# Two-block model on one core: the first panel of each feed-forward as an ordinary product

## The reference

```
x = x + nsa_pool_mixer(rmsnorm(x))        # attention in three branches, multiscale pooling, w_out
x = x + swiglu(rmsnorm(x), w_gate, w_up, w_down)                  # feed-forward 1
x = x + conformer_conv(rmsnorm(x))        # 31-tap depthwise convolution, layernorm, silu
x = x + swiglu(rmsnorm(x), ...)                                   # feed-forward 2
x = rmsnorm(x)
x = x + gla_and_short_conv(rmsnorm(x))    # gated linear attention in chunks, 3-tap convolution
x = x + swiglu(rmsnorm(x), ...)                                   # feed-forward 3
x = x + sigmoid(rmsnorm(x) @ w_ple_gate) * (p @ w_ple_proj);  out = rmsnorm(x)
swiglu(h) = (silu(h @ w_gate) * (h @ w_up)) @ w_down              # 1024 -> 2816 -> 1024
```

## Time and profile before

| | us |
|---|---|
| time before, median of 3 runs | 1819.22 (1817.42 to 1821.11) |
| the profiled execution's own time | 1818.26 |
| its span, first to last instruction | 1816.5 |
| TensorE busy | 1727.3 (95%) |
| VectorE busy | 1284.4 (71%) |
| ScalarE busy | 882.8 (49%) |
| GpSimd busy | 557.9 (31%) |
| mean granted TensorE clock, share of full | 0.973 |

### The profile page before, as it was taken

One profiled execution on the slowest core, in us unless ns is written; L12 is line 12 of the kernel. 1 busy time (PEld: TensorE's weight loads), 2 busy tenths in 40 slices (PEclk: granted clock), 3 DMA queues, 4 the chain that ended last, 5 costly groups with the idle time before them and its releaser, 6 DMA issues.

```text
span 1816.5 us, 28182 instructions
## 1 busy us (share of the span) xinstructions
PE 1727.3 (95%) x10884; PEld 1503.3 (83%) x10884; DVE 1284.4 (71%) x1818; ACT 882.8 (49%) x1368; POOL 557.9 (31%) x392
## 2 busy tenths in 40 slices
PE   7989988999999999988999999999998899999997
PEld 6767778988998865778988998788777898899876
DVE  8667687754775798787754876678868775477575
ACT  5328566732673312556732673432246674277342
POOL 1332124512540246234502540024502451255000
PEclk9899999999999999989999999999998999999998
DMA  6210223433333465222433332322211343333322
GB/s 213 79 47 2 70 59 81 117 103 93 107 87 100 120 156 146 70 70 73 114 105 104 94 102 85 122 70 70 90 50 49 92 115 96 93 111 90 113 88 75
DMA packets 284702, 169.04 MB, mean 93 GB/s; under 512 B 8288, under 2 KB 278528, under 8 KB 284576
## 3 DMA queue, kind: packets, MB, share of 16 engines
q1 hardware_dynamic: 283664, 165.10, 32.4%
q0 software_dynamic: 624, 1.67, 0.3%
q10 hardware_dynamic: 288, 0.54, 0.1%
HBM read 156.59 MB, written 2.10 MB: 87 GB/s over the span
## 4 chain that ended last, share of the span: by engine, by line
PE 84%; DVE 10%; ACT 3%; issue 3%; DMA 1%; POOL 0%; SPq 0%; DVEq 0%; ACTq 0%; POOLq 0%
PE ps L1324 36%; PE ps L1012 13%; PE ps L1013 13%; PE ps L1014 13%; PE ps L1391 1%; PE ps L1250 1%; DVE wlo L1614 1%; PE ps L1207 1%; PE ps L1232 1%; DVE ps L2131 1%; DVE rstd L1656 1%; ACT act_hi L611 1%; DVE sqacc L1634 1%; DVE tt L1951 1%; DMA raw<-in_nsa_w_in_dram 1%
## 5 line engine op out<-in xcount | busy, mean ns | idle before, releaser
L1012 PE MATMUL ps<-act_hi,whi 128*128 128x512 f32 x700 | 281.4, 402 | 18.4 <-DVE act_lo L1646 8.4
L1013 PE MATMUL ps<-act_lo,whi 128*128 128x512 f32 x700 | 276.0, 394 | 0.0
L1014 PE MATMUL ps<-act_hi,wlo 128*128 128x512 f32 x700 | 275.9, 394 | 0.0
L602 ACT ACTIVATE whi<-raw 128x2048 fp32r<-128x2048 f32 (+3 forms) x98 | 155.6, 1587 | 239.8 <-PE ps L1014 226.1
L1012 PE MATMUL ps<-hid_hi,whi 128*128 128x512 f32 x528 | 209.8, 397 | 0.0
L1013 PE MATMUL ps<-hid_lo,whi 128*128 128x512 f32 x528 | 209.8, 397 | 0.0
L1014 PE MATMUL ps<-hid_hi,wlo 128*128 128x512 f32 x528 | 209.8, 397 | 0.0
L1614 DVE TENSOR_TENSOR wlo<-raw,whi 128x2048 fp32r<-128x2048 f32 (+3 forms) x90 | 177.6, 1973 | 35.7 <-ACT whi L602 35.4
L440 POOL TENSOR_TENSOR raw<-raw 128x512 f32<-128x512 f32 x66 | 86.2, 1307 | 364.6 <-DMA raw<-in_ffn_w_up_dram 217.1
L1012 PEld LDWEIGHTS ps<-act_hi,whi 128*128 128x128 f32 x700 | 133.5, 191 | 58.1 <-issue 21.6
L450 POOL TENSOR_TENSOR raw<-raw,ssum 128x512 f32<-128x512 f32 x66 | 105.4, 1597 | 247.8 <-DVE wlo L1925 247.8
(11 more groups left out here) (403 smaller groups left out, 4370.0 us busy)
## 6 DMA issues: line engine op xcount, KB each, us to landing
raw<-in_ffn_w_gate_dram SPq DMA_DIRECT2D x44, 512.0 KB, 3.9
raw<-in_ffn_w_up_dram SPq DMA_DIRECT2D x44, 512.0 KB, 5.1
raw<-in_w_gate_upffn_dram SPq DMA_DIRECT2D x44, 512.0 KB, 4.4
raw<-in_ffn_w_down_dram SPq DMA_DIRECT2D x32, 384.0 KB, 3.8
raw<-in_conv_w_pw_dram SPq DMA_DIRECT2D x24, 512.0 KB, 5.7
raw<-in_w_in_dram SPq DMA_DIRECT2D x24, 512.0 KB, 4.7
raw<-in_ffn_w_down_dram SPq DMA_DIRECT2D x32, 320.0 KB, 3.6
z<-z SPq DMA_DIRECT2D x28, 262.0 KB, 5.0
```

Of the source, the lines that this page charges most:

```text
L602: act.activation(whi[:, n % 2, 0:cols], raw[:, n % 2, 0:cols], ACT.Copy).then_inc(hi_done, 1)
L1012: pe.matmul(out, lhs[0], rhs[0], start=start, stop=False)
L1013: pe.matmul(out, lhs[0], rhs[1], start=False, stop=False)
L1014: return pe.matmul(out, lhs[1], rhs[0], start=False, stop=stop)
```

## The change

Five edits; everything else in the diff renumbers semaphores (one `act` and one `xhi` counter for all stages, `seven(u)` for the count of seven-product units).

1. Unit 0 of each feed-forward is made by ordinary products: 8 blocks x 2 outputs x 3 matmuls of 512 columns, with the whole normed x in `act_hi` and `act_lo`. GpSimd makes no weight sums for it, ScalarE no `take`; VectorE scales the gate (`whole_gate`) and multiplies (`whole_hidden`) over 512 columns.
2. B11, B21 and B22 of the later units are read out of `act_hi` and `act_lo` where they lie; T4 is written over the fourth quarter once panel 0 is done. T1, T2, T3 have tiles of their own.
3. `late` is ordered anew: T2 and T3 of the first two blocks, then T1, then panel 0's split, the casts of all blocks at k = 7 behind `act_free`, panel 1's split, the last sums and T2 and T3.
4. Attention: all four pool groups ahead of `second_scores(0)`, `pooled` on ScalarE, the second pair's second scores and the third pair's first scores moved around the first transposes.
5. Linear attention: the three tap products per block on ScalarE (`tap_products`), GpSimd keeps two sums and a product.

```diff
@@ TensorE, feed-forward
                     for k in ks:
                         u, n = KF * f + k, N0[up_] + k - ks[0]
                         a, b, c = up_banks(dn, u)
+                        if k == 0:
+                            pe.wait_ge(split_done, n + 1)
+                            for kk in range(KD):
+                                if kk == 5:
+                                    sumsq(q)
+                                pe.wait_ge(*act_of(q)(kk))
+                                for half, out in enumerate((a, b)):
+                                    ins = mm3(out[:, :], slot(n, half * KD + kk, P), act_k(kk), kk == 0, kk == KD - 1)
+                            ins.then_inc(panel_done, 1)
+                            continue
...
-                        if k > ks[0]:
+                        if k > ks[0] and k != 1:
                             fourth(u - 1, n - 1)
+                        if k == 1:
+                            pe.wait_ge(sem("bt_lo"), 10 * f + 9)
@@ ScalarE, late
                 for k in range(KD):
-                    if k % 2 == 0 and k < KD - 2 and k // 2 >= ahead:
+                    if k % 2 == 0 and k // 2 >= ahead:
                         hi(N0[name] + k // 2 + 1)
...
+                    if k == KD - 1:
+                        for kk in range(KD - 1):
+                            act.wait_ge(sem("act_free"), 7 * use + kk + 1)
+                            cast(act_hi[:, kk], x[:, kk], "xhi", gain(q, kk))
+                    act.wait_ge(bank_free, T0[name] + k + 5)
+                    if k == KD - 1:
+                        act.wait_ge(panel_done, N0[name] + 4)
+                        cast(act_hi[:, k], x[:, k], "xhi", gain(q, k))
+                    square(q, k, x[:, k])
+                    if Q4 <= k < KD - 2:
+                        part("T2", k - Q4)
+                        part("T3", k - Q4)
+                    if k == KD - 3:
+                        cast(flat2(combo("T1")[0]), flat2(n1[:, :, :]), "bt_hi", -1.0)
+                hi_panel(u0 + 1, n0 + 1)
+                for i in (2, 3):
+                    part("T2", i)
+                    part("T3", i)
@@ ScalarE, feed-forward
+                        if k == 0:
+                            root(q)
+                            act.wait_ge(sem("std_ready"), q + 1)
+                            hi_sum(u + 1, n + 1, dn, 0)
+                            continue
...
                         take(u, dn, 0)
+                        if k == 1:
+                            act.wait_ge(panel_done, n)
+                            act.wait_ge(sem("bt_sum"), 16 * f + 16)
+                            cast(combo("T4")[0], tt4[:, :, :], "bt_hi")
@@ VectorE, late
+                    if k == KD - 1:
+                        low_norm(q, k - 1)
+                        low_norm(q, k)
                     add_square(q, k)
...
                     if k == KD - 2:
+                        for kk in range(KD - 2):
+                            low_norm(q, kk)
+                lo_panel(u0 + 1, n0 + 1)
+                for i in (2, 3):
+                    summed(i)
+                for i in (2, 3):
+                    part("T2", i)
+                    part("T3", i)
@@ VectorE, feed-forward
+                        if k == 1:
+                            lo_sum(u, dn, 0)
+                            inv(q)
+                            lo_sum(u, dn, 1)
+                            whole_gate(u - 1, n - 1)
+                            lo_sum(u, dn, 2)
+                            low(combo("T4")[1], tt4[:, :, :], combo("T4")[0], "bt_hi", 10 * f + 10, "bt_lo")
+                            lo_panel(u + 1, n + 1)
+                            gate_first(u)
+                            whole_hidden(u - 1)
+                            low_hidden(u - 1)
+                            gate_second(u)
+                            continue
@@ TensorE, attention
             pool_groups((0, 1))
+            pe.wait_ge(sem("cmp_act"), 4)
+            pool_groups((2, 3))
             second_scores(0)
-            pe.wait_ge(sem("cmp_dve"), 7)
-            pe.wait_ge(sem("cmp_act"), 3)
-            pool_groups((2, 3))
             first_scores(1)
-            second_scores(1)
             pe.wait_ge(bank_free, T0["pool"] + 8)
             for p in range(pairs):
                 transposed(p, 0)
-                if p + 2 < pairs:
+                if not p:
+                    second_scores(1)
+                elif p + 2 < pairs:
                     first_scores(p + 2)
                 transposed(p, 1)
                 if p:
                     weighted(p - 1)
+                else:
+                    first_scores(2)
@@ GpSimd, short_conv
-                pool.wait_ge(sem("ccx_ready"), k + 1)
-                for tap in range(3):
-                    col = COL["conv_w_2"] + tap * 4 + k
-                    own.link(pool.tensor_tensor(t3[:, min(tap, 1)], ccx[:, k % 2, tap:tap + S],
-                                                par[:, col:col + 1].broadcast_to([P, S]), ALU.mult))
-                    if tap:
-                        own.link(pool.tensor_tensor(t3[:, 0], t3[:, 0], t3[:, 1], ALU.add))
-                pool.tensor_tensor(cbt[:, k], cbt[:, k], t3[:, 0], ALU.mult).then_inc(sem("yc_ready"), 1)
+                pool.wait_ge(sem("tap_ready"), 3 * (k + 1))
+                own.link(pool.tensor_tensor(sq[:, 0], sq[:, 0], sq[:, 1], ALU.add))
+                own.link(pool.tensor_tensor(sq[:, 0], sq[:, 0], t3[:, 0], ALU.add))
+                pool.tensor_tensor(cbt[:, k], cbt[:, k], sq[:, 0], ALU.mult).then_inc(sem("yc_ready"), 1)
@@ ScalarE, linear attention (called behind the decays of levels 4 and 5, behind ebc, and behind g2's first split)
+            def tap_products(k):
+                act.wait_ge(sem("ccx_ready"), k + 1)
+                if k:
+                    act.wait_ge(sem("yc_ready"), k)
+                for tap, dst in enumerate((sq[:, 0], sq[:, 1], t3[:, 0])):
+                    col = COL["conv_w_2"] + tap * 4 + k
+                    act.activation(dst, ccx[:, k % 2, tap:tap + S], ACT.Copy, scale=par[:, col:col + 1])\
+                        .then_inc(sem("tap_ready"), 1)
+            act.wait_ge(sem("yc_ready"), 4)
```

More of the change, by code:

```diff
@@ L788, in late @@
-                    act.wait_ge(bank_free, T0[name] + k + 5)
-                    if k < Q4:
-                        part("B11", k, k)
-                    else:
-                        part("B21", k - Q4, k)
-                        part("T2", k - Q4, k)
-                    square(q, k, x[:, k])
-                act.wait_ge(panel_done, N0[name] + 4)
-                for i in range(Q4):
-                    part("B22", i, Q4 + i)
-                act.wait_ge(sem("bt_sum"), 16 * f + 15)
-                cast(flat2(combo("T3")[0]), flat2(tt3[:, :, :]), "bt_hi")
@@ L835, in ffn @@
                             silu(u - 1)
-                        if not first:
+                            take(u, dn, 2)
                             cast_hidden(u - 1)
-                        take(u, dn, 2)
-                        if k == 0:
-                            root(q)
-                            act.wait_ge(sem("std_ready"), q + 1)
+                        else:
+                            if not first:
+                                cast_hidden(u - 1)
+                            take(u, dn, 2)
                         if k < ks[-1]:
@@ L962, in _ @@
             hi(N0["g2"] + 1)
+            tap_products(3)
             gate_tile(0)
@@ L1314, in ffn, with product @@
                     up_, dn = up + part, down + part
-                    def product(out, w, name, start, sig, entry):
+                    def product(out, w, name, start, sig):
                         b_hi, b_lo = combo(name)
                         for k in range(Q4):
-                            if entry:
-                                pe.wait_ge(sem("bt_lo"), 19 * f + combo_count(name, k))
                             w_hi, w_lo = w(k)
@@ L1649, in low_norm @@
             def low_norm(q, k):
-                low(act_lo[:, k], x[:, k], act_hi[:, k], f"xhi{q}", k + 1, f"act{q}", gain(q, k))
+                low(act_lo[:, k], x[:, k], act_hi[:, k], "xhi", ACTS[q] + k + 1, "act", gain(q, k))
             def inv(q):
@@ L1883, in low_output @@
                 low(act_lo[:, k], acc[:, k], act_hi[:, k], "o_hi", k + 1, "o_lo")
[L1885 to L1898 removed]
+            shift_first(0, 0)
+            shift_first(0, 1)
+            shift_second(0)
+            shift_first(1, 0)
+            shift_first(1, 1)
             for p in range(pairs):
                 copy_pt(p, 0)
[L1901 removed]
+                if not p:
+                    shift_second(1)
+                    copy_pt(p, 1)
+                    shift_first(2, 0)
+                    shift_first(2, 1)
+                    factors(p)
+                elif p + 2 < pairs:
                     shift_first(p + 2, 0)
@@ L2086, in ffn @@
```

(2 more changed lines are left out.)

253 lines of the change are left out of this document (117 added, 136 removed).

## The result

The changed kernel takes 1806.3 us (median of 8 runs, 1802.9 to 1813.1) beside 1819.6 for the kernel before (8 runs): the ratio is 0.9927, with a 95% interval of 0.9912 to 0.9942. That is 13.4 us faster, where 28 were forecast. It lies inside the range, but less than half of the gain came. The profiled execution took 1802.9 us, its span is 1801.1 (before 1816.5).

A forecast was written before the change was run, and what follows sets the result against it. TensorE, busy for 95% of the span, was taken as the bound, with only its holes to win. Feed-forwards 3 x 6.5, attention 5 and taps 3 sum to 27.5 us off 1818.3: 1791 us predicted, range 1773 to 1807.

The forecast's parts named there:

- The failed step: Feed-forward from panel 3 on: the same seven products and reads as before, so no gain and no loss.
- Panel 0, the matmuls: First panel of each feed-forward: 48 wide matmuls replace 84 narrow ones, 1.05 us more each, 3 us in all.
- Panel 0, what it waits for: Feed-forward entry, laid out hole by hole up to panel 3: 8.0 us gained, less 1.5 for clock, 6.5 per feed-forward.
- Attention: Attention's first pairs: second pair's transposes 6.0 us earlier, less 1 for the clock, so 5 us.
- Tap products: Linear attention's levels: tap products on ScalarE disturb VectorE for half the time, 3 us of a possible 4.3.
- rival 2: Feed-forward entries: the hole moves to late casts and half clock, 2.5 us each; 12.5 us in all, 1806; chance 13%.
- rival 1: Panel 1: covers hold, holes shrink to about half, 11 us per feed-forward; 42 us in all, 1776; chance 22%.
- rival 3: Feed-forward entry: VectorE becomes the bound; at 10 us late each loses 2, so slower, 1824; chance 4%.
- rival 4: Feed-forwards give 6.5 each, attention and tap products nothing, as ScalarE's longer queue eats them; 1799; chance 13%.

The follow-up runs named there:

- slots reversed: The changed kernel with the three slots of the combined activations in reverse order (T3 in slot 0, T1 in slot 2): 1809.8 us (one run).
- mixed: The changed kernel with paddings of 64, 64 and 32 bytes ahead of hidden blocks, combinations and summed weights: 1797.5 us, ratio 0.9878 to the kernel before.
- placed starts: The changed kernel with hidden blocks and combinations starting 192 bytes later, summed weights 384 bytes later: 1787.3 us, ratio 0.9826 to the kernel before.
- all starts in phase: The changed kernel with 64 bytes of padding ahead of the feed-forward's own buffers (hidden blocks, combinations, summed weights): 1813.1 us (one run).
- without the additions: The changed kernel without GpSimd's two additions of the tap products per block, so the short convolution is not computed: 1803.7 us (one run).
- table of pairs: TensorE alone, the changed kernel's panel with all 64 pairs of shifts of combinations and summed weights: 9.840 us per panel at the best pair.

## Why the prediction was half right

**The failed step** is the one sentence "From panel 3 on nothing changes: the same seven products, the strided activation blocks are read as 256 contiguous columns each as before." The instructions are the same, but four products changed where they read: B11 and B21 went from the combinations' tensor (192 modulo 256) to act (128), T1 and T3 the other way. By the table above that is, per twelve matmuls, +0.056, +0.025, -0.022 and +0.062 us: +0.12 per panel, 7.5 us over 63. A hint stood in the trace of before: 0.117 is the mean of 828 narrow products, and single products had 113 and 120; I took the mean for a property of the width. Of the 12.1 us between the forecast sum and the spans' 15.4, the panels are 7.5, the taps 2.1, attention 1.6 and the stretches with unchanged instructions 2.1; the entries gave 1.2 more than forecast.

**Panel 0, the matmuls.** 1.05 us more per feed-forward; 0.2265 per wide product fits (227.4).

**Panel 0, what it waits for.** Right in its mechanism and nearly in size. Attention had moved everything 3.2 us earlier; with that taken off, my layout says T1 259.7, B21 263.0, B22 267.9, and the trace 259.81, 262.86, 267.95. In part this closeness is luck: the layout's own terms for T1 add up to 262.6, not to the 262.9 that it goes on with. The holes are 1.6, 1.8, 1.4, 2.0 and 2.0, sum 8.7 against 9.3 (panel 0 and panel 2 waited longer, T1 and B21 shorter, and the hole before T4 did not come). The clock was charged at 1.5; over 268 to 276 it is 0.79, which is 1.7 us. Gain 6.3, 7.1 and 7.3 in the three feed-forwards, forecast 6.5 each.

**Attention: mis-sized term.** The first factors came 4.9 us earlier (144.17 to 139.25; forecast 6.0). But the next interval is 9.75 long instead of 8.19, its clock 0.83 where before it was 1.00: 0.17 x 9.75 = 1.7 us, and 3.4 stay of them. I had charged 1 for the clock. Even the 3.4 came only in some executions. The stretch from 130 to 150 us (columns as in the earlier trace rows) in the changed kernel, then in the one with the slots reversed, whose instructions there are the same:

```profile
130.00:150.00 20.00, 16.44 (x148) 12.86 (x148) 14.56 (x59) 15.68 (x52) 3.11 (x3) 0.91 0.00 1
...
130.00:150.00 20.00, 16.82 (x108) 13.95 (x110) 11.64 (x45) 13.74 (x45) 2.04 (x2) 0.66 0.00 1
```

With a clock of 0.91 mix begins at 198.97 (198.86 and 198.41 in the kernels with mixed and with placed starts, same clock), with 0.66 at 202.60 (202.60 with all starts in phase, 202.58 without the additions); in the kernel before it was 202.36. So this part gives 3.4 to 4.0 us or nothing, as the clock falls. That also is a part of the changed kernel's spread over 10 us. What decides it no run shows.

**Tap products: mis-sized term.** Forecast 3, 0.9 came. The possible gain was 3.5, not 4.3: the starts of the levels in the trace of before are 13.92, 13.91, 14.03, 15.29 and 16.02 apart, so the two late ones cost 1.4 and 2.1, not 1.2 and 3.1. The layout's premise, VectorE disturbed for half the time, was too kind. GpSimd is still busy for 8.9 of the 16 us ahead of level 4: it waits for ScalarE's third product until 1243.36, 10.3 us ahead of the level where it began 14.6 ahead before, and so the end of its work stays 1.1 us ahead of the level, as before. Its last product and its difference for the next decay take 3.22 and 2.76 us beside the split and the two products on which the level waits (3.27, 1.71, 2.91 us), each to 0.01 us as in the kernel before. Level 4 is 15.37 long as before (15.29), only level 5 won 1.0.

**The rivals.** The result, 1806.3, is the number of rival 2, with a chance of 0.13, and that is a coincidence: its mechanism did not come, no hole moved. That the result lies inside the range is luck as well, since no term of the range was the panels'. The covers (rival 1) did not hold, VectorE did not become the bound (rival 3), and rival 4 is wrong in that the small parts gave something. None of the rivals had a price for the steady panels, which are more than a third of TensorE's time (63 x 9.9 = 627 of 1729 us).

## What to carry to other kernels

When an edit moves operands to other buffers, price every matmul that reads them, also where the instructions are unchanged: 0.12 us per panel are 7.5 us over 63 panels. Where TensorE is the bound, lay out the start addresses modulo 256 bytes on purpose: a short kernel that runs TensorE alone at the real addresses reproduced the panel to a nanosecond and found in one run a padding worth as much as the rewrite. And work that is taken off GpSimd wins little as long as the end of its queue still falls beside the VectorE operation that is waited for: look at what stands last in the queue, not at how much was taken out.

## What the runs showed of the hardware

- The pitch of a matmul depends on the starts of activations and weights modulo 256 bytes: with TensorE alone and one pair of starts throughout, 256 columns take 120 ns when equal, 120 also with the activations 96 bytes beyond, and 117 to 119 otherwise; 512 columns take 227 when equal, otherwise 229 to 234. For narrow products equal starts are the slowest, for wide ones the fastest. In the panels, where the pairs change every twelve matmuls, narrow products take 113 to 120, equal ones 118 to 120.
- What decides between 113 and 118 at one and the same difference stays open. B21 of the kernel before takes 113.3 when it directly follows B11 (run so with TensorE alone) and 118 in its place in the panel; a product often takes four to seven matmuls until its pitch is steady (B21 of the changed panel, TensorE alone: 127, 118, 125, 113, 119, then 120 ns). So shifts can't simply be added, and the table of pairs had to be measured.
- ScalarE and VectorE, both over 95% busy, cost TensorE nothing (5.66 us for 48 matmuls with and without them); GpSimd at work beside it costs VectorE 1.7 us in a product of 1.2.
- The granted clock of the same instructions differs between executions: 0.91 or 0.66 over 130 to 150 us in attention, worth 3.6 us.
